# Stage heads of a two-block transformer kernel reordered: who turns, copies and splits the tokens between stages

## The reference, cut to what matters

```python
def first_block(x, ...):      # deepnorm, layer norm after each sublayer
    x = layer_norm(ALPHA * x + even_mixer(x))       # ev: SSD scan and stick-breaking attention
    x = layer_norm(ALPHA * x + hier_moe(x))         # m0: 16 experts, 4 groups, top 2
    x = layer_norm(ALPHA * x + odd_mixer(x))        # od: latent attention and forgetting attention
    x = layer_norm(ALPHA * x + hier_moe(x))         # m1
def second_block(h, ...):     # RMS norm before each sublayer
    h = h + spatial_gating_mixer(rmsnorm(h))        # sg
    h = h + swiglu(rmsnorm(h))                      # ff: dense, 2816 hidden
    h = h + diff_attention(rmsnorm(h), positions)   # da
    h = h + moe_swiglu(rmsnorm(h))                  # m2: 8 experts, 3584 hidden, top 2
```

## Time and profile before

| what | value |
|---|---|
| runs | 2284.41, 2285.02, 2277.63 us; median 2284.41 |
| profiled execution | 2285.4 us, span 2283.7 us |
| mean granted TensorE clock | 0.967 |
| busy: PE, PEld | 2142.7 us (94%), 1734.1 us (76%) |
| busy: DVE, ACT, POOL | 1748.5 us (77%), 1429.6 us (63%), 77.7 us (3%) |
| chain that ended last | PE 78%, DVE 11%, issue 5%, ACT 4%, DMA 1% |

### The profile page before, as it was taken

The page is one execution under the profiler, slowest core; times in us unless marked ns, Lnnn a source line. Parts: engine busy times, 40 slices in busy tenths (PEclk is TensorE's granted clock), DMA queues, the critical chain, the costliest instruction groups (busy, mean ns, idle before and its releaser), DMA issues.

```text
span 2283.7 us, 31475 instructions
## 1 busy us (share of the span) xinstructions
PE 2142.7 (94%) x9970; PEld 1734.1 (76%) x9970; DVE 1748.5 (77%) x2353; ACT 1429.6 (63%) x1919; POOL 77.7 (3%) x72
## 2 busy tenths in 40 slices
PE   8998998998997998999897899999999999999998
PEld 7974776875775786888674687878888787878786
DVE  4654898755988666545766698989898998989897
ACT  5662775442774544444452687878788787878785
POOL 0001000001000000111111000000000000000000
PEclk9998999998998998999998899999999999999999
DMA  6315784232883435552230798989889898989895
GB/s 249 120 68 231 294 332 184 100 145 113 367 323 127 166 148 230 206 213 78 112 147 1 310 373 320 378 318 381 345 351 373 324 380 319 376 322 373 322 384 205
DMA packets 81400, 577.11 MB, mean 253 GB/s; under 512 B 9392, under 2 KB 9392, under 8 KB 12848
## 3 DMA queue, kind: packets, MB, share of 16 engines
q1 hardware_dynamic: 79744, 570.40, 63.6%
q0 software_dynamic: 1584, 5.77, 0.7%
HBM read 575.08 MB, written 1.05 MB: 252 GB/s over the span
## 4 chain that ended last, share of the span: by engine, by line
PE 78%; DVE 11%; issue 5%; ACT 4%; DMA 1%; DVEq 0%; POOL 0%; SPq 0%; ACTq 0%; POOLq 0%
PE bank L465 22%; PE bank L467 21%; PE bank L466 21%; PE bank L923 2%; PE bank L1396 2%; DVE h L1754 1%; PE bank L1362 1%; PE bank L587 1%; PE bank L2776 1%; DVE gu_lo L1702 1%; DVE dn_lo L1702 1%; DVE pj_lo L502 1%; PE bank L1435 1%; ACT gu_hi L1531 1%; ACT dn_hi L1539 1%
## 5 line engine op out<-in xcount | busy, mean ns | idle before, releaser
L1702 DVE TENSOR_TENSOR gu_lo<-ffw_gu,gu_hi 128x1024 fp32r<-128x1024 f32 x620 | 755.4, 1238 | 90.5 <-ACT gu_hi L1531 76.0
L1531 ACT CAST gu_hi<-ffw_gu 128x1024 fp32r<-128x1024 f32 x620 | 648.3, 1053 | 101.2 <-PE bank L467 69.2
L465 PE MATMUL bank<-gu_hi,xg_lo 128*128 128x512 f32 x1152 | 462.9, 402 | 5.0 <-DVE xg_lo L1702 4.5
L467 PE MATMUL bank<-gu_hi,xg_hi 128*128 128x512 f32 x1152 | 452.2, 393 | 0.0
L466 PE MATMUL bank<-gu_lo,xg_hi 128*128 128x512 f32 x1152 | 451.3, 392 | 0.0
L1702 DVE TENSOR_TENSOR dn_lo<-ffw_d,dn_hi 128x1024 fp32r<-128x1024 f32 x299 | 362.8, 1222 | 58.1 <-ACT dn_hi L1539 48.7
L1539 ACT CAST dn_hi<-ffw_d 128x1024 fp32r<-128x1024 f32 x310 | 325.3, 1056 | 96.6 <-PE bank L467 92.9
L465 PE MATMUL bank<-dn_hi,hidt_lo 128*128 128x512 f32 x664 | 265.7, 400 | 29.2 <-DVE hidt_lo L1702 29.2
L467 PE MATMUL bank<-dn_hi,hidt_hi 128*128 128x512 f32 x664 | 259.6, 391 | 0.0
L466 PE MATMUL bank<-dn_lo,hidt_hi 128*128 128x512 f32 x664 | 259.6, 391 | 0.0
L465 PEld LDWEIGHTS bank<-gu_hi,xg_lo 128*128 128x128 f32 x1152 | 217.6, 189 | 48.5 <-DVE xg_lo L1702 5.3
(11 more groups left out here) (410 smaller groups left out, 2807.0 us busy)
## 6 DMA issues: line engine op xcount, KB each, us to landing
ffw_gu<-in_gate_up_m SPq DMA_DIRECT2D x288, 1024.0 KB, 6.9
ffw_d<-in_down_m SPq DMA_DIRECT2D x144, 1024.0 KB, 7.7
pieces<-in_pieces SPq DMA_DIRECT2D x70, 1024.0 KB, 7.1
ffw_gu<-in_gate_up_ff SPq DMA_DIRECT2D x22, 1024.0 KB, 6.9
ffw_d<-in_down_ff SPq DMA_DIRECT2D x11, 1024.0 KB, 8.9
pieces<-in_pieces SPq DMA_DIRECT2D x4, 512.0 KB, 8.3
norm_vec<-in_ln_g POOLq DMA_DIRECT2D x4, 512.0 KB, 4.0
norm_vec<-in_ln_b POOLq DMA_DIRECT2D x4, 512.0 KB, 4.9
```

Source lines behind the costliest of these rows:

```text
L465: nc.tensor.matmul(bank, a_lo, b_hi, start=start, stop=False)
L467: return nc.tensor.matmul(bank, a_hi, b_hi, start=False, stop=stop)
L1531: nc.scalar.copy(gu_hi[:, 2 * k:2 * k + 2, :], ffw_gu[:, blk["slot"], 2 * k:2 * k + 2, :])\
L1702: return V.tensor_tensor(out, x, hi.bitcast(F32), ALU.subtract)
```

## The change: order and owners in the stage heads

In words: (1) in m0 and m1 ScalarE copies the turned features, tile 0 ahead of the token casts and tile 1 behind them, and waits for `h` itself; VectorE no longer does. (2) `tok_lo` of all three routed stages is made by VectorE, not GpSimd. (3) `layer_norm_begin` is split, and in the heads of od and sg the centring of tile 1 stands behind tile 0's features and low part. (4) `project_first_tensor` turns tile 1 in the middle of tile 0's products. (5) The turn of tile 0 for ff and for m2 stands inside the out product of sg and da; ff's tile 1 is turned in the middle of its tile 0's first products. (6) VectorE's list at the head of ff: features and low part of tile 0 right behind its add, sums of tile 0 behind the add of tile 1, sums of tile 1 last; ScalarE waits for the second root only before its second token tile. (7) m2's features of tile 0 come ahead of its norm, and its casts wait for the normed tile alone. (8) da's setup moves into sg: VectorE's two halves at `at` = 7 and 11, ScalarE's behind piece 1.

```diff
     def layer_norm_begin(j):
+        layer_norm_ask(j)
+        layer_norm_center(j)
+    def layer_norm_ask(j):
         tile_moments(j)
         vlink(V.tensor_scalar(sq[:, j:j + 1], moments[:, j, 1:2], LN_EPS, None, ALU.add))
         root_ask_vector()
+    def layer_norm_center(j):
         vlink(V.scalar_tensor_tensor(out=h[:, j, :], in0=h[:, j, :], scalar=moments[:, j, 0:1], in1=norm_vec[:, 0:D],
...
+    def features_tile_scalar(act, t, j):
+        for b in range(2):
+            turned_wait(act, t, j, b)
+            ins = nc.scalar.copy(xT[:, 4 * b:4 * b + 4, TILES[j]], turned(t, j, b))
+        ins.then_inc(sem("xt_tile"), 1)
...
     def project_first_tensor(pe, t, first_bank):
+        turn_tile_tensor(pe, t, 0)
         for j in range(T):
-            turn_tile_tensor(pe, t, j)
             for k in range(4):
...
+                if j == 0 and k == 2:
+                    turn_tile_tensor(pe, t, 1)
                 for c in (2 * k, 2 * k + 1):
...
     def route_tensor(pe, t, route):
         for j in range(T):
-            turn_tile_tensor(pe, t, j)
+            if j or t != "m2":
+                turn_tile_tensor(pe, t, j)
...
     def dense_tensor(pe):
-        for j in range(T):
-            turn_tile_tensor(pe, "ff", j)
         pe.wait_ge(sem("xt_split"), 1)
...
         gate_up_tensor(pe, first, x_of(first), 0)
+        turn_tile_tensor(pe, "ff", 1)
         gate_up_tensor(pe, first, x_of(first), 1)
...
     def ff_scalar(act, t):
...
-            act.wait_ge(sem("rms_ready"), 4)
+            act.wait_ge(sem("rms_ready"), 3)
         else:
+            if t != "m2":
+                features_tile_scalar(act, t, 0)
             for j in range(T):
-                turned_wait(act, t, j, 1)
                 if t == "m2":
                     act.wait_ge(sem("normed"), j + 1)
+                else:
+                    tile_wait(act, t, j)
                 nc.scalar.copy(tok_hi[:, j, :], (normed if t == "m2" else h)[:, j, :]).then_inc(sem("tok_hi_ready"), 1)
+            if t != "m2":
+                features_tile_scalar(act, t, 1)
...
             down_hi_scalar(act, first, 1)
+            act.wait_ge(sem("rms_ready"), 4)
             hidt_hi_scalar(act, middle(act, t, 0, step))
...
     def ff_gpsimd(pool, t):
...
-        if t != "ff":
-            for j in range(T):
-                pool.wait_ge(sem("tok_hi_ready"), T * ROUTER[t] + j + 1)
-                g.tensor_tensor(tok_lo[:, j, :], ..., ALU.subtract).then_inc(sem("tok_ready"), 1)
...
+    def tok_lo_vector(dve, t, j):
+        dve.wait_ge(sem("tok_hi_ready"), T * ROUTER[t] + j + 1)
+        rest(tok_lo[:, j, :], (normed if t == "m2" else h)[:, j, :], tok_hi[:, j, :]).then_inc(sem("tok_ready"), 1)
...
     def route_vector(dve, t, bias):
...
             best_two(sem("route_member"))
             exponents()
+            tok_lo_vector(dve, t, 1)
...
     def routed_tiles_vector(dve, t, i):
...
         layer_norm_begin(1)
-        features_tile_vector(t, 0, None, sem("xt_tile"))
         layer_norm_end(1)
         dve.sem_inc(sem("phase_done"), 1)
-        features_tile_vector(t, 1, None, sem("xt_tile"))
+        for j in range(T):
+            tok_lo_vector(dve, t, j)
...
     def moe_first_vector(dve, t, i):
...
-        layer_norm_begin(1)
+        layer_norm_ask(1)
         if t == "m1":
             features_tile_vector("sg", 0, par["l0_mix_norm_2"], sem("xt_chunks"))
         x_lo_tile_vector(NEXT[t], 0)
+        layer_norm_center(1)
         layer_norm_end(1)
...
     def sg_tensor(pe):
...
+                    if j and i == 3 and c == 1:
+                        turn_tile_tensor(pe, "ff", 0)
...
     def sg_scalar(act):
...
+            if n == 1:
+                da_setup_scalar(act)
...
         first_weights_scalar(act, "ff")
-        da_setup_scalar(act)
...
     def sg_vector(dve):
...
+                if at == 7:
+                    da_setup_begin_vector(dve)
+                if at == 11:
+                    da_setup_end_vector(dve)
...
         first_weights_vector(dve, "ff")
-        da_setup_vector(dve)
         gain = par["l0_ffn_norm_2"]
         out_add_vector("sg", 0, 1.0, sem("h_ready"))
-        rms_begin(0)
-        rms_end()
+        features_tile_vector("ff", 0, gain, sem("xt_tile"))
+        x_lo_dense_vector(dve, 0)
         out_add_vector("sg", 1, 1.0, sem("h_ready"))
         dve.sem_inc(sem("phase_done"), 1)
-        features_tile_vector("ff", 0, gain, sem("xt_tile"))
+        rms_begin(0)
+        features_tile_vector("ff", 1, gain, sem("xt_tile"))
+        rms_end()
+        x_lo_dense_vector(dve, 1)
         rms_begin(1)
-        x_lo_dense_vector(dve, 0)
         rms_end()
-        features_tile_vector("ff", 1, gain, sem("xt_tile"))
-        x_lo_dense_vector(dve, 1)
...
     def moe_second_vector(dve):
...
         rms_begin(0)
+        features_tile_vector("m2", 0, gain, sem("xt_tile"))
         normed_tile_vector(0)
         out_add_vector("da", 1, 1.0, sem("h_ready"))
         dve.sem_inc(sem("phase_done"), 1)
-        features_tile_vector("m2", 0, gain, sem("xt_tile"))
         rms_begin(1)
         features_tile_vector("m2", 1, gain, sem("xt_tile"))
+        tok_lo_vector(dve, "m2", 0)
         normed_tile_vector(1)
...
     def da_tensor(pe):
...
                 last = da_out_tensor(1, j, half, range(4))
+                if j and half == 0:
+                    turn_tile_tensor(pe, "m2", 0)
```

More of the change, by code:

```diff
@@ L1689, in step @@
                 down_lo(st)
-        if t != "ff":
-            for j in range(T):
-                pool.wait_ge(sem("tok_hi_ready"), T * ROUTER[t] + j + 1)
-                g.tensor_tensor(tok_lo[:, j, :], (normed if t == "m2" else h)[:, j, :], tok_hi[:, j, :].bitcast(F32),
-                                ALU.subtract).then_inc(sem("tok_ready"), 1)
         if t == "ff":
@@ L2928, in da_setup_scalar, with da_setup_begin_vector @@
         A.activation(lam_sum, lam_sum, ACT.Exp).then_inc(sem("da_terms"), 1)
-    def da_setup_vector(dve):
+    def da_setup_begin_vector(dve):
         two_pi = 2 * math.pi
@@ L2951, in da_setup_vector, with da_setup_end_vector @@
             vlink(V.memset(par["da_columns"][first:first + ROT], 1.0))
+    def da_setup_end_vector(dve):
         dve.wait_ge(sem("da_terms"), 1)
```

## The result

The changed kernel takes 2252.05 us (median of four runs, 2251.79 to 2256.09), the kernel before 2281.11 on the same chip (four runs, 2277.63 to 2285.02): a ratio of 0.9868, with a 95% interval of 0.9851 to 0.9885, or 29.1 us (26 to 34). The forecast was 28.2 us and 2256.2; of the 4.2 us between that and 2252.05, 3.3 lie in the median of the kernel before, which was 2284.41 with three runs and 2281.11 with four. The two profiled executions lie further apart, 33.7 us by their spans (2283.7 and 2250.0).

The account below looks back on a forecast made before the run. TensorE bounds the kernel (busy 94%), and the change works only on the seven stage heads, where it waits or runs at half clock. Terms 8.4 + 2.4 + 3.9 + 0 + 10.2 + 1.3 + 2.0 = 28.2: 2256.2 us, range 2249 to 2266.

Parts of the forecast that it names:

- m0, m1: Heads of routed stages m0 and m1: logits read earlier with ScalarE making the feature copies, 4.2 us each, 8.4 together.
- od: Head of od: earlier first product and tile 1's turn inside tile 0's products gain 2.4 us, bounds 1.5 and 2.9.
- sg: Head of sg: earlier start and earlier turn of tile 1 gain 3.9 us, bounds 2.5 and 4.3.
- Setup inside sg: Angle setup moved from sg's end in among its pieces: costs nothing there, up to 1.5 us if the lead is short.
- the rival of the slow switch: In sg, function switches of about 2.66 us make TensorE wait at piece 3, 1.5 to 2.8 us: 2258.5; chance 0.10.
- a TensorE wait inside a stage for pj_lo: Sign that the prediction is wrong: TensorE waiting within a stage for the low part of a projection piece.
- ff: Head of ff: first product 10.5 us earlier, 9.5 left behind the second root, plus 0.7: 10.2, bounds 8.5 and 11.
- da: Head of da: turning tile 1 after 12 products instead of 24 gains 1.3 us, bounds 1.0 and 1.4.
- m2: Head of m2: earlier routing and no GpSimd subtractions beside the ranking gain 2.0 us, bounds 1.0 and 3.1.
- the clock stays up: Rival, in the heads: smaller TensorE gaps let routing, gather and first products run at full clock, up to 2246; chance 0.07.
- The rival of half gains: In the heads: waits move to ScalarE's casts and copies and ff's second root, gain 18 us, 2266; chance 0.12.
- the slower one: Rival, in m2's loop: each of 112 blocks 0.3 us later, +34 us, net +6, 2290; chance 0.03.

Follow-up runs that it names:

- copies_vector: Changed kernel with the feature copies of m0 and m1 back on VectorE in the old order, low parts staying on VectorE: 2262.63 us, ratio 0.9912.
- switches: Changed kernel with one extra Sin and one extra Exp on ScalarE ahead of the angle setup, so two more function switches in sg: 2257.51 us, ratio 0.9882.
- ff_first_vector: Changed kernel with both low parts of ff's first down piece on VectorE, the hidden low part between them, GpSimd first at the third block: 2255.75 us, ratio 0.9874.
- turn_late: Changed kernel with tile 1's turn again behind all 24 products of tile 0 in the heads of od, sg and da: 2256.01 us, ratio 0.9875.
- ff_list_back: Changed kernel with VectorE's list at the head of ff in its old order, setup staying inside sg and turns as changed: 2260.81 us, ratio 0.9915.

## Why the prediction was right, and where it was off

The mechanism and the bound held: the gain is in the heads. The sum was 28.2; the heads of the profiled executions give 28.8, the medians 29.1. That these agree so closely is in part luck: sg's error of 1.1 and m2's of 0.4 are set against ff's of 0.6 and small ones, and on another chip the medians lie 32.5 apart (2284.14 and 2251.68). Term by term:

- **m0, m1**: 4.2 each predicted, 3.9 and 4.3 found. Cast and copies ran in the order assumed (the logits are ready at 211.2, with tile 1's routing from 207.63 at half clock). `copies_vector` confirms the cause.
- **od**: 2.4 predicted, 2.3 found. The turn at 402.25 met a tile that had been normed at 400.89, and tile 1's products follow without a wait.
- **sg**: 3.9 predicted, 5.0 found, the largest error. The places were right: the wait of 2.02 is gone and one of 1.46 before piece 1 has come (forecast 1.7). The mis-sized term is the turn's start, on which VectorE's whole row hangs: "4.0 earlier" was 5.1 (745.30 before, 728.03 after, less the shift of 12.21 at the stage's entry), since I let all 12 products ahead of it run at half clock and only seven did (0.8, net of a slower first product and a start 0.1 later), and since I had read the turn's start before as 745.07, which is that of the last product ahead of it (0.2).
- **Setup inside sg**: 0 predicted and found; the lead was 1.46 us, not 1.3. `switches` prices it: the rival of the slow switch is refuted. The prediction's sign of being wrong, "a TensorE wait inside a stage for pj_lo", is there at piece 1 (1.46), but its own sum has this wait at 1.7; the sign holds for sg's other pieces, and they have none (da's of 0.74 at 1082.73 was 0.79 before).
- **ff**: 10.2 predicted, 9.6 found. The first product came 10.5 earlier and the hidden product's turn 9.4 (9.5 forecast). The term that failed is "I give half of that, 0.7": GpSimd's subtraction now starts together with VectorE's, which stands still for the whole of it, so the gain behind the root was some 0.2 us. `ff_first_vector`, which takes GpSimd's subtraction away, gets 1.9 us there.
- **da**: 1.3 and 1.3. VectorE was busy with tile 1's sums and the root rather than with waiting for the turn, so TensorE still waits 0.51. `turn_late` adds a condition: where tile 0's products run at full clock, the turn's place gives nothing.
- **m2**: 2.0 predicted, 2.4 found: routing 1.0 and the ranking step 1.4, as forecast; less 0.6, since the gather waits 1.08 for the second low part where it waited 0.45 before; and 0.6 for the turns of the gathered tokens, at full clock now and at half clock before.

The rival "the clock stays up" had a share, the 5 us estimated above, in ff, m2 and sg. Tile 1's routing, though, ran at half clock as before (3.60), so it did not decide; tile 0's ran at full clock (1.96), but off the path. The rival of half gains falls with `copies_vector` and `ff_list_back`, the slower one with the shift of 33.5 at both ends of m2's loop. What I had not reckoned with is the noise between two executions: 4.8 of the 33.7 us lie in stretches that the diff leaves alone, nearly all of it more or fewer products at half clock.

## What to carry to other kernels

Read a head by asking which instruction releases the bound engine next, and hand that engine's late operand to whoever has been idle longest; a copy of 0.57 us on an idle ScalarE was worth 3.8 us a stage here. An idle TensorE often costs twice: behind waits of 5.57 and 6.82 us the next seven and twelve products ran at half clock. It is no rule that these traces give: behind the same wait of 3.26 us in da, eight products ran at half clock in the changed kernel and none in `turn_late`. And when an effect is a few us in 2250, compare the same instruction's start in two traces before trusting a median.

## What was not expected of the hardware

- A VectorE instruction with two SBUF inputs that starts beside a running GpSimd subtraction stands still until that ends, however small it is (0.18 became 1.89; 1.23 became 3.51 beside 2.42); one with a single input does not (0.17).
- The same program, with TensorE busy throughout, was granted 0.54 in one execution and 0.86 in another over the same 12 us, worth 4 us of run time.
